# A state-space scan's decay tiles: exponents of both directions joined before one exponential

## The chip, the cores and the metric

One core of one Trainium2 chip runs the whole program. The metric is the device time of one execution in microseconds (us), the median of several runs. TensorE (PE) multiplies matrices, VectorE (DVE), ScalarE (ACT) and GpSimd (POOL) work on elements, SyncE (SP) issues the weight loads.

## The reference, cut to what matters

Two transformer-like blocks over 256 tokens of width 1024. The part of this case is the first block's bidirectional state-space scan: 8 groups of 4 heads, two chunks of 128 tokens, one scan forwards and one backwards over the same `b`, `c` and `x`:

```python
decay = segsum_exp(a_dt)      # exp(cs[l] - cs[s]) where l >= s, else 0
cb = jnp.einsum('bclgn,bcsgn->bcgls', c, b)
y_diag = jnp.einsum('bcgls,bcgrls,bcsgrp->bclgrp', cb, decay, xdt)
...
y = y_fwd + y_bwd + xs * d_skip.astype(jnp.float32).reshape(G, R, 1)
```

With s on the partitions and l along the free axis, the forward scan fills the entries l >= s of a tile, the backward scan the entries l <= s, and both fill the diagonal l = s, where the exponential of each is 1 (times its own dt).

## The kernel before, in words

All weights come as a stream of 147 pieces of 1 MB. Piece s belongs to slot s. For each slot SP loads `raw`, ACT copies it rounded to `w_hi` (`split_hi`, L1068), DVE subtracts (`w_lo`, `split_lo`, L1452), and PE multiplies the activations with both, three products each (`three`, L393). PE handles slot s in two halves of 12 matmuls of 512 columns each. ACT and DVE run two slots ahead (`AHEAD = 2`) with their splits: in their loop over s they split piece s + 2, and ACT may do so once PE has finished slot s - 1. Each engine follows its own list in program order and waits only on semaphores.

The scan lies in slots 27 to 36, the last of the z projection and the first of the gate projection; group g is worked on in slot 28 + g. Each PSUM bank has a pair of counters: PE `claim`s a bank by waiting until its last user has drained it; `ready` waits until PE has filled it, `emptied` until it is drained. For every group:

- After slot 27 + g, PE computes `ssd_cb(g)` (L884, bank 7) and `ssd_decay(g, 0)`; in the middle of slot 28 + g it computes `ssd_decay(g, 1)` (`slot_middle`, L897), and after that, for group g - 1, `ssd_states` (L852), `ssd_diagonal` (L843, bank 4) and `ssd_across` (L893, bank 7).
- `ssd_decay(g, c)` writes the exponents of a tile of 128 x 512 (4 heads) for the forward direction into bank 5 and for the backward one into bank 6. For each it issues a matmul of `cum_s` with `cum_l` (L865), and a second one (L867) that adds -1e30 on the half that the direction does not have: `unit` (an identity) times `far` (the mask).
- ACT copies `cb` (L1227), takes the exponentials of both banks for c = 0 (`decay_exps`, L1149, L1157), splits the weights of slot s + 2, does the squares of group g - 2 (L1316), the exponentials for c = 1, and the copy of `state` (L1323). In slots 28 and 30 it also applies Silu to a z chunk (L1329), so its function tables are exchanged.
- DVE in slot 28 + g: `ssd_weigh(g, 0)` (L1702: add the two exponentials, L1706, multiply with `cb`, L1709), `split_lo` (L1455), `ssd_weigh(g, 1)`, `ssd_gate(g - 1)` (L1713: times `d_skip`, L1720; `y_off`, L1724, which frees bank 7 for the next `ssd_cb`; three more, L1728 to L1736), and after every second gate slot `gate_bias` (L1743).
- POOL makes `x_state` (L2069) and the rows `cum_s` of the next group (L2078).

Of the kernel before, what the change touches and what calls it, by code (L numbers as in the profile page):

```python
# [33 lines left out]
P = 128  # L34
TOK = 256
# [112 lines left out]
def build(nc, w_stream, w_dt, x_in, params_in, table_in, onehot_in, gate_bias_in, post_in, rpb_in,  # L148
# [3 lines left out]
    with ctx:  # L152
# [106 lines left out]
        decay_back = [at(f"decay_back{c}", [P, PER_GROUP, P], 150592 + 2048 * c) for c in range(RT)]  # L259
        cb = at("cb", [P, RT, P], 154688)  # L260
        far = at("far", [P, 2, P], 141376, F32R)
        ndt = at("ndt", [P, RT, 2 * HEADS], 158272)
        unit = at("unit", [P, P], 158784, F32R)
# [68 lines left out]
        decay_scaled, far_ready, x_state_ready = sem("decay_scaled"), sem("far_ready"), sem("x_state_ready")  # L332
# [40 lines left out]
        def _(pe):  # L373
# [482 lines left out]
            def ssd_decay(g, c):  # L856


                pe.wait_ge(cum_s_ready, g + 1)
                if g == 0 and c == 0:  # L860
                    pe.wait_ge(far_ready, 1)
                for d in range(2):
                    key = ("decay", g, c, d)
                    claim(key, 5 + d)
                    pe.matmul(ps[:, 5 + d, :], cum_s[g % 2][:, 2 * c + d, :], cum_l[c][:, d, :, :],  # L865
                              start=True, stop=False)
                    pe.matmul(ps[:, 5 + d, :], unit[:, :], far[:, d].unsqueeze(1).to_broadcast([P, PER_GROUP, P]),  # L867
                              start=False, stop=True).then_inc(*fill_of(key))
# [28 lines left out]
            def slot_middle(s):  # L897

                if 0 <= s - 10 < 8:
                    values1(s - 10)  # L900
                if 0 <= s - 97 < 4:
                    values2(s - 97)
                if s in TURN_AT:
                    conv_turn(TURN_AT[s])
                if 0 <= s - 28 < GROUPS:
                    ssd_decay(s - 28, 1)
                if 0 <= s - 29 < GROUPS:
                    ssd_states(s - 29)
                    ssd_diagonal(s - 29)
                    ssd_across(s - 29)  # L910
# [148 lines left out]
        def _(act):  # L1059
# [89 lines left out]
            def decay_exps(g, c):  # L1149
                for d, dest in enumerate((decay[g % 2][c], decay_back[c])):  # L1150
                    key = ("decay", g, c, d)
                    ready(act, key)
                    if d == 0 and g >= 2:
                        ready(act, ("y", g - 2))
                    if d == 1 and g:
                        act.wait_ge(decay_scaled, 2 * g - 1 + c)
                    act.activation(dest[:, :, :], ps[:, 5 + d, :].rearrange("p (h l) -> p h l", h=PER_GROUP),  # L1157
                                   ACT.Exp).then_inc(*drain_of(key))
# [60 lines left out]
            for s in range(SLOTS):  # L1219
                if 0 <= s - 28 < GROUPS:  # L1220
                    g = s - 28
                    key = ("cb", g)
                    ready(act, key)
                    if g:

                        act.wait_ge(decay_scaled, 2 * g)
                    act.activation(cb[:, :, :], ps[:, 7, 0:2 * P].rearrange("p (c l) -> p c l", c=2),  # L1227
                                   ACT.Copy).then_inc(*drain_of(key))
                    decay_exps(g, 0)
# [3 lines left out]
                if s == S_Q2 - 2:  # L1233
                    split_hi(S_Q2 + 1)
                name, form, chunk, part, opens, closes = slots[s]
# [82 lines left out]
                if 0 <= s - 28 < GROUPS:  # L1318
                    decay_exps(s - 28, 1)
                if 0 <= s - 29 < GROUPS:  # L1320
# [3 lines left out]
                                   ACT.Copy).then_inc(*drain_of(key))  # L1324
                if name == "z" and closes:
# [117 lines left out]
        def _(dve):  # L1443
# [257 lines left out]

            def ssd_weigh(g, c):  # L1702

                emptied(dve, ("decay", g, c, 0)), emptied(dve, ("decay", g, c, 1))
                w = decay[g % 2][c]
                link(dve.tensor_tensor(w[:, :, :], w[:, :, :], decay_back[c][:, :, :], ALU.add))  # L1706
                if c == 0:
                    emptied(dve, ("cb", g))
                dve.tensor_tensor(w[:, :, :], w[:, :, :],  # L1709
                                  cb[:, c, :].unsqueeze(1).to_broadcast([P, PER_GROUP, P]),  # L1710
                                  ALU.mult).then_inc(decay_scaled, 1)

            def ssd_gate(g):  # L1713
# [4 lines left out]
                for c in range(RT):  # L1718
                    v = xtok(c, g * GW, GW).rearrange("p (h d) -> p h d", h=PER_GROUP)
                    ins = dve.tensor_tensor(v, v, per_head(param("d_skip")[:, 4 * g:4 * g + 4], 4), ALU.mult)  # L1720
                link(ins)
                ready(dve, ("off", g))
# [97 lines left out]
            for s in range(SLOTS):  # L1820
                if 0 <= s - 28 < GROUPS:
                    ssd_weigh(s - 28, 0)
# [61 lines left out]
                if s == 18:  # L1884
                    decay_tables()
                if 0 <= s - 28 < GROUPS:
                    ssd_weigh(s - 28, 1)
# [149 lines left out]
        def _(pool):  # L2037
# [36 lines left out]
            def decay_rows(g):  # L2074

                if g >= 2:
                    ready(pool, ("decay", g - 2, 1, 0))
# [4 lines left out]
            pool.tensor_copy(unit[:, :], ident)  # L2082
# [3 lines left out]
            pool.wait_ge(conv_silu, 7)  # L2086
            pool.tensor_scalar(far[:, :, :], tri[:, 2:4], NEG, None, ALU.mult).then_inc(far_ready, 1)
# [14 lines left out]
            ready(pool, ("decay", GROUPS - 1, 1, 0))  # L2102
# [128 lines left out]
```

## Time and profile before

| | us |
|---|---|
| median of 3 runs | 943.63 (942.15 to 943.77) |
| the profiled execution | 942.23 |
| its span, first to last instruction | 940.4 |
| PE busy | 932.4 (99%) |
| DVE busy | 662.4 (70%) |
| ACT busy | 507.6 (54%) |
| POOL busy | 60.8 (6%) |

An instruction's duration is not the distance to the next one: matmuls and element operations overlap their neighbours' ends. Where many of one kind follow each other, the distance from start to start is what one of them costs its engine. An f32 matmul (not rounded) has two records in the trace. Only one execution has a trace, and its times are given from the start of its span.

### The profile page before, as it was taken

The page shows a single profiled execution, that of the slowest core. Times are in us where ns is not written, and L with a number is a line of the kernel's source. Part 1 is how long each engine was busy: PE and PEld are TensorE (multiplying, and loading weights), DVE is VectorE, ACT ScalarE, POOL GpSimd, SP SyncE. Part 2 cuts the span into 40 slices and gives each one's busy share as a digit, 9 for nine tenths or more (in the row PEclk, how much of TensorE's full clock was granted, in tenths as well). Part 3 has the DMA queues.
Part 4 walks back from the last instruction along what each step waited for, and adds up shares of the span by engine and source line. Part 5 has one row for each costly group of instructions (what it writes and reads, how often), then busy time and mean ns, then how long its engine had stood idle before and what let it go on. Part 6 is the DMA issues. An engine that isn't in the chain of part 4 may idle for free.

```text
span 940.4 us, 13246 instructions
## 1 busy us (share of the span) xinstructions
PE 932.4 (99%) x5362; PEld 807.9 (86%) x5362; DVE 662.4 (70%) x946; ACT 507.6 (54%) x664; POOL 60.8 (6%) x68
## 2 busy tenths in 40 slices
PE   9999999999999999999999999999999999999998
PEld 8988899988888888888888888899888898888887
DVE  6779789998878764778776446767665758776433
ACT  6457876676555733456554335755653455554331
POOL 1000000023321000000003310000000000000000
PEclk9999999999999999999999999999999999999999
DMA  8943233554224475435447955353355435546551
GB/s 306 341 168 124 93 133 135 180 167 169 91 90 157 140 307 197 169 131 221 179 180 236 256 196 206 136 205 128 123 217 179 179 135 217 187 179 224 178 179 45
DMA packets 25278, 166.51 MB, mean 177 GB/s; under 512 B 2987, under 2 KB 3115, under 8 KB 6657
## 3 DMA queue, kind: packets, MB, share of 16 engines
q1 hardware_dynamic: 22464, 156.12, 46.1%
q0 software_dynamic: 2752, 9.54, 3.5%
q8 instruction: 43, 0.70, 0.3%
q14 instruction: 19, 0.15, 0.0%
HBM read 164.57 MB, written 1.08 MB: 176 GB/s over the span
## 4 chain that ended last, share of the span: by engine, by line
PE 86%; DVE 11%; ACT 2%; issue 1%; ACTq 0%; DVEq 0%
PE ps L393 54%; PE ps L582 11%; PE ps L587 6%; DVE conv_acc L1688 5%; DVE w_lo L1455 3%; PE ps L843 1%; PE ps L772 1%; PE ps L787 1%; PE ps L424 1%; PE ps L426 1%; PE ps L433 1%; PE ps L512 1%; PE ps L630 1%; PE ps L893 1%; PE ps L852 1%
## 5 line engine op out<-in xcount | busy, mean ns | idle before, releaser
L1455 DVE TENSOR_TENSOR w_lo<-raw,w_hi 128x2048 fp32r<-128x2048 f32 x145 | 331.3, 2291 | 181.0 <-ACT w_hi L1075 180.8
L1075 ACT ACTIVATE w_hi<-raw 128x2048 fp32r<-128x2048 f32 x145 | 275.5, 1906 | 179.1 <-PE ps L393 160.2
L393 PE MATMUL ps<-w_hi,ht 128*128 128x512 f32 (+1 forms) x576 | 181.4, 388 | 0.0
L393 PE MATMUL ps<-ht,w_hi 128*128 128x256 f32 (+1 forms) x816 | 150.6, 286 | 0.0
L393 PEld LDWEIGHTS ps<-ht,w_hi 128*128 128x128 f32 (+1 forms) x816 | 126.2, 190 | 4.1 <-issue 4.0
L393 PEld LDWEIGHTS ps<-w_hi,ht 128*128 128x128 f32 x576 | 107.3, 188 | 22.4 <-issue 1.1
L393 PE MATMUL ps<-ht,w_lo 128*128 128x256 f32 (+1 forms) x408 | 115.3, 282 | 0.0
L393 PE MATMUL ps<-w_lo,ht 128*128 128x512 f32 (+1 forms) x288 | 110.5, 384 | 0.0
L582 PE MATMUL ps<-ht,w_hi 128*128 128x512 f32 x448 | 109.5, 391 | 0.0
L393 PE MATMUL ps<-w_hi,ff_hi 128*128 128x512 f32 x256 | 99.7, 389 | 0.0
L393 PE MATMUL ps<-w_lo,ff_hi 128*128 128x512 f32 x256 | 99.6, 389 | 0.0
L393 PE MATMUL ps<-w_hi,ff_lo 128*128 128x512 f32 x256 | 99.6, 389 | 0.0
L582 PEld LDWEIGHTS ps<-ht,w_hi 128*128 128x128 f32 x448 | 81.5, 189 | 15.2
L393 PEld LDWEIGHTS ps<-ht,w_lo 128*128 128x128 f32 (+1 forms) x408 | 77.6, 190 | 0.0
L393 PEld LDWEIGHTS ps<-w_lo,ht 128*128 128x128 f32 x288 | 54.2, 188 | 10.4
L587 PEld LDWEIGHTS ps<-ht,w_lo 128*128 128x128 f32 x448 | 59.3, 191 | 3.3
L587 PE MATMUL ps<-ht,w_lo 128*128 128x256 f32 x448 | 60.3, 282 | 0.0
L393 PEld LDWEIGHTS ps<-w_hi,ff_hi 128*128 128x128 f32 x256 | 48.1, 188 | 10.0
L393 PEld LDWEIGHTS ps<-w_hi,ff_lo 128*128 128x128 f32 x256 | 48.0, 188 | 10.0
L393 PEld LDWEIGHTS ps<-w_lo,ff_hi 128*128 128x128 f32 x256 | 48.1, 188 | 9.8
L1688 DVE SCALAR_TENSOR_TENSOR conv_acc<-conv_in,params,conv_acc 128x256 f32<-128x256 f32 x128 | 52.1, 477 | 0.0
L1190 ACT ACTIVATE ff_sum<-ps 128x512 f32<-128x512 f32 x32 | 18.8, 595 | 35.4 <-PE ps L587 34.4
(301 smaller groups left out, 1217.4 us busy)
## 6 DMA issues: line engine op xcount, KB each, us to landing
raw<-in_w_stream SPq DMA_DIRECT2D x145, 1024.0 KB, 4.8
bias<-rel_scratch POOLq DMA_DIRECT2D x1, 3072.0 KB, 21.2
bias<-in_rpb POOLq DMA_DIRECT2D x16, 128.0 KB, 7.9
x_first<-in_x_in SPq DMA_DIRECT2D x2, 512.0 KB, 4.1
raw<-in_w_stream SPq DMA_DIRECT2D x2, 512.0 KB, 6.4
gates<-in_gate_bias POOLq DMA_DIRECT2D x4, 256.0 KB, 6.0
gates<-in_gate_bias POOLq DMA_DIRECT2D x2, 512.0 KB, 7.2
x<-in_x_in POOLq DMA_DIRECT2D x1, 1024.0 KB, 5.3
```

Of the source, the lines that this page charges most:

```text
L393: ins = pe.matmul(o, still, moving, start=first and n == 0, stop=last and n == 2, skip_group_check=True)
L424: pe.matmul(ps[:, i, 0:TOK], hi[:, c], ht_hi[:, k, :], start=opens and kt == 0, stop=False, skip_group_check=True)
L426: pe.matmul(ps[:, i, 0:TOK], lo[:, c], ht_hi[:, k, :], start=False, stop=False, skip_group_check=True)
L433: ins = pe.matmul(ps[:, i, TOK:2 * TOK], hi[:, kt * 512 + i * P:kt * 512 + i * P + P], ht_lo[:, 4 * part + kt, :], start=False, stop=close ...
L512: pe.matmul(ps[:, bank0 + r, :], ht_hi[:, 4 * part + kt, tokens], w[:, kt * 512:kt * 512 + 512], start=part == 0 and kt == 0 and m == 0, s ...
L582: pe.matmul(ps[:, 4 * (chunk % 2) + i, :], hi[:, cols(kt, i)], ht[:, :, 4 * part + kt, :], start=opens and kt == 0, stop=False, skip_group ...
L587: ins = pe.matmul(ps[:, 4 * (chunk % 2) + i, 0:TOK], lo[:, cols(kt, i)], ht_hi[:, 4 * part + kt, :], start=False, stop=closes and kt == 3, ...
L630: pe.matmul(ps[:, 2 * n + r, :], a_hi[:, kt, r * P:r * P + P], w[:, cols], start=kt == 0 and m == 0, stop=False, skip_group_check=True)
L1075: act.activation(split_home(s)[0][:, 0:width(s)], raw[s % RAW_RING][:, 0:width(s)], ACT.Copy).then_inc(hi_ready, 1)
L1190: act.activation(ff_sum[half][:, :, :], ps[:, b:b + 2, TOK:2 * TOK], ACT.Copy).then_inc(lows_out, 1)
L1455: dve.tensor_tensor(lo[:, 0:width(s)], raw[s % RAW_RING][:, 0:width(s)], hi[:, 0:width(s)].bitcast(F32), ALU.subtract).then_inc(lo_ready, 1)
L1688: ins = dve.scalar_tensor_tensor(acc_of(c)[:, i, :], conv_in[k][:, i, tap:tap + TOK], conv_w[:, tap, f:f + 1], acc_of(c)[:, i, :], ALU.mul ...
```

## The change

Bank 5 gets the forward exponents and bank 6 the backward ones, with no mask product. DVE copies bank 6 over bank 5 where s > l (`ssd_choose`, a predicated copy with the mask `tri[:, 2]`), which drains bank 6. ACT then takes one exponential of bank 5, which drains it, and DVE multiplies with `cb`; the add is gone. The diagonal now holds the forward share alone. The backward share is `dt` of the backward direction times the row product of b and c: DVE multiplies b and c once (`twins`, 128 x 2048), 16 matmuls of one column sum over the partitions (`twin_sums`, bank 4), and `own_terms` adds the result to `d_skip`, giving `own_skip`, by which `ssd_gate` multiplies in place of `d_skip`. On ACT the exponential for c = 0 now stands behind the weight split of its slot, and the one for c = 1 behind the copy of `state`. On DVE the multiplication for c = 1 moves into `ssd_gate` of the group before, behind its skip product. POOL no longer makes `unit` and `far`.

```diff
@@ -256,11 +256,10 @@
         gates = at("gates", [P, RT, 2 * D], 192352)
         decay = [[at(f"decay{i}_{c}", [P, PER_GROUP, P], 142400 + 4096 * i + 2048 * c) for c in range(RT)]
                  for i in range(2)]
-        decay_back = [at(f"decay_back{c}", [P, PER_GROUP, P], 150592 + 2048 * c) for c in range(RT)]
+        twins = at("twins", [P, GROUPS, TOK], 146496)
         cb = at("cb", [P, RT, P], 154688)
-        far = at("far", [P, 2, P], 141376, F32R)
         ndt = at("ndt", [P, RT, 2 * HEADS], 158272)
-        unit = at("unit", [P, P], 158784, F32R)
+        own_skip = at("own_skip", [P, RT, HEADS], 158784)
 
         adt_wide = at("adt_wide", [P, 4, 4, HEADS], 175968)
         ndt_wide = at("ndt_wide", [P, 4, 4, HEADS], 184160)
@@ -857,15 +856,22 @@
 
 
                 pe.wait_ge(cum_s_ready, g + 1)
-                if g == 0 and c == 0:
-                    pe.wait_ge(far_ready, 1)
                 for d in range(2):
                     key = ("decay", g, c, d)
                     claim(key, 5 + d)
                     pe.matmul(ps[:, 5 + d, :], cum_s[g % 2][:, 2 * c + d, :], cum_l[c][:, d, :, :],
-                              start=True, stop=False)
-                    pe.matmul(ps[:, 5 + d, :], unit[:, :], far[:, d].unsqueeze(1).to_broadcast([P, PER_GROUP, P]),
-                              start=False, stop=True).then_inc(*fill_of(key))
+                              start=True, stop=True).then_inc(*fill_of(key))
+
+            def twin_sums():
+
+                claim("twins", 4)
+                pe.wait_ge(twins_ready, 1)
+                for c in range(RT):
+                    for g in range(GROUPS):
+                        at0 = c * GROUPS + g
+                        ins = pe.matmul(ps[:, 4, at0:at0 + 1], twins[:, g, c * P:c * P + P], tri[:, 0, P - 1:P],
+                                        start=True, stop=True)
+                ins.then_inc(*fill_of("twins"))
 
             def cumulate():
 
@@ -904,6 +910,8 @@
                     conv_turn(TURN_AT[s])
                 if 0 <= s - 28 < GROUPS:
                     ssd_decay(s - 28, 1)
+                    if s == 28:
+                        twin_sums()
                 if 0 <= s - 29 < GROUPS:
                     ssd_states(s - 29)
                     ssd_diagonal(s - 29)
@@ -1147,15 +1155,14 @@
                 ins.then_inc(exp_ready, 1)
 
             def decay_exps(g, c):
-                for d, dest in enumerate((decay[g % 2][c], decay_back[c])):
-                    key = ("decay", g, c, d)
-                    ready(act, key)
-                    if d == 0 and g >= 2:
-                        ready(act, ("y", g - 2))
-                    if d == 1 and g:
-                        act.wait_ge(decay_scaled, 2 * g - 1 + c)
-                    act.activation(dest[:, :, :], ps[:, 5 + d, :].rearrange("p (h l) -> p h l", h=PER_GROUP),
-                                   ACT.Exp).then_inc(*drain_of(key))
+                key = ("decay", g, c, 0)
+                emptied(act, ("decay", g, c, 1))
+                if g == 1 and c == 0:
+                    ready(act, "twins")
+                if g >= 2:
+                    ready(act, ("y", g - 2))
+                act.activation(decay[g % 2][c][:, :, :], ps[:, 5, :].rearrange("p (h l) -> p h l", h=PER_GROUP),
+                               ACT.Exp).then_inc(*drain_of(key))
 
             def values_hi(a):
                 r, tile = a // 4, 2 * (a % 4)
@@ -1226,12 +1233,13 @@
                         act.wait_ge(decay_scaled, 2 * g)
                     act.activation(cb[:, :, :], ps[:, 7, 0:2 * P].rearrange("p (c l) -> p c l", c=2),
                                    ACT.Copy).then_inc(*drain_of(key))
-                    decay_exps(g, 0)
                 late = s in (S_MI - 1, S_MI2 - 1)
                 if s + AHEAD < SLOTS and s != S_Q2 - 1 and not late:
                     split_hi(s + AHEAD)
                 if s == S_Q2 - 2:
                     split_hi(S_Q2 + 1)
+                if 0 <= s - 28 < GROUPS:
+                    decay_exps(s - 28, 0)
                 name, form, chunk, part, opens, closes = slots[s]
                 if s == 0:
                     ready(act, "rel")
@@ -1315,13 +1323,13 @@
                             act.wait_ge(gsq_ready, 2 * g + c)
                         act.activation(junk[:, :], xtok(c, g * GW, GW), ACT.Square,
                                        accum_out=gstat[:, 0, 2 * g + c:2 * g + c + 1]).then_inc(gsq_ready, 1)
-                if 0 <= s - 28 < GROUPS:
-                    decay_exps(s - 28, 1)
                 if 0 <= s - 29 < GROUPS:
                     key = ("state", s - 29)
                     ready(act, key)
                     act.activation(state[:, :, :], ps[:, 7, :].rearrange("p (a b) -> p a b", a=2),
                                    ACT.Copy).then_inc(*drain_of(key))
+                if 0 <= s - 28 < GROUPS:
+                    decay_exps(s - 28, 1)
                 if name == "z" and closes:
                     for r in range(RT):
                         key = ("z", chunk, r)
@@ -1699,16 +1707,35 @@
 
                 return values.unsqueeze(2).to_broadcast([P, count, HD])
 
+            def ssd_choose(g, c):
+
+                ready(dve, ("decay", g, c, 0)), ready(dve, ("decay", g, c, 1))
+                both = [ps[:, 5 + d, :].rearrange("p (h l) -> p h l", h=PER_GROUP) for d in range(2)]
+                dve.copy_predicated(both[0], tri[:, 2].bitcast(I32).unsqueeze(1).to_broadcast([P, PER_GROUP, P]),
+                                    both[1]).then_inc(*drain_of(("decay", g, c, 1)))
+
             def ssd_weigh(g, c):
 
-                emptied(dve, ("decay", g, c, 0)), emptied(dve, ("decay", g, c, 1))
-                w = decay[g % 2][c]
-                link(dve.tensor_tensor(w[:, :, :], w[:, :, :], decay_back[c][:, :, :], ALU.add))
+                emptied(dve, ("decay", g, c, 0))
                 if c == 0:
                     emptied(dve, ("cb", g))
+                w = decay[g % 2][c]
                 dve.tensor_tensor(w[:, :, :], w[:, :, :],
                                   cb[:, c, :].unsqueeze(1).to_broadcast([P, PER_GROUP, P]),
                                   ALU.mult).then_inc(decay_scaled, 1)
+
+            def own_terms():
+
+                ready(dve, "twins")
+                v = own_skip[:, :, :].rearrange("p c (g h) -> p c g h", g=GROUPS)
+                for c in range(RT):
+                    ins = dve.tensor_tensor(v[:, c], dt[:, c, HEADS:2 * HEADS].rearrange("p (g h) -> p g h", g=GROUPS),
+                                            ps[:, 4, c * GROUPS:c * GROUPS + GROUPS].unsqueeze(2)
+                                            .to_broadcast([P, GROUPS, PER_GROUP]), ALU.mult)
+                ins.then_inc(*drain_of("twins"))
+                emptied(dve, "twins")
+                link(dve.tensor_tensor(own_skip[:, :, :], own_skip[:, :, :],
+                                       param("d_skip").unsqueeze(1).to_broadcast([P, RT, HEADS]), ALU.add))
 
             def ssd_gate(g):
 
@@ -1717,8 +1744,10 @@
                 dve.wait_ge(x_state_ready, 2 * (g + 1))
                 for c in range(RT):
                     v = xtok(c, g * GW, GW).rearrange("p (h d) -> p h d", h=PER_GROUP)
-                    ins = dve.tensor_tensor(v, v, per_head(param("d_skip")[:, 4 * g:4 * g + 4], 4), ALU.mult)
+                    ins = dve.tensor_tensor(v, v, per_head(own_skip[:, c, 4 * g:4 * g + 4], 4), ALU.mult)
                 link(ins)
+                if g + 1 < GROUPS:
+                    ssd_weigh(g + 1, 1)
                 ready(dve, ("off", g))
                 for i in range(RT):
                     ins = dve.tensor_tensor(y_off[:, i].rearrange("p (h d) -> p h d", h=PER_GROUP),
@@ -1819,7 +1848,7 @@
 
             for s in range(SLOTS):
                 if 0 <= s - 28 < GROUPS:
-                    ssd_weigh(s - 28, 0)
+                    ssd_choose(s - 28, 0)
                 if 0 <= s - 10 < 8:
                     values_lo(s - 10)
                 if s in TURN_AT:
@@ -1883,8 +1912,16 @@
                                     .unsqueeze(2).to_broadcast([P, 4, 2, HEADS])).then_inc(adt_wide_ready, 1)
                 if s == 18:
                     decay_tables()
+                if s == 27:
+                    dve.wait_ge(conv_silu, 8)
+                    dve.tensor_tensor(twins[:, :, :], bc[:, 0:GROUPS, :], bc[:, GROUPS:2 * GROUPS, :],
+                                      ALU.mult).then_inc(twins_ready, 1)
                 if 0 <= s - 28 < GROUPS:
-                    ssd_weigh(s - 28, 1)
+                    ssd_weigh(s - 28, 0)
+                    ssd_choose(s - 28, 1)
+                if s == 28:
+                    ssd_weigh(0, 1)
+                    own_terms()
                 if s == S_GATE + 5:
                     dve.wait_ge(gate_bias_second, 32)
                     gate_bias(1)
@@ -2074,17 +2111,14 @@
             def decay_rows(g):
 
                 if g >= 2:
-                    ready(pool, ("decay", g - 2, 1, 0))
+                    ready(pool, ("decay", g - 2, 1, 1))
                 pool.tensor_scalar(cum_s[g % 2][:, :, :], cum[:, :, :], quad[:, 10 + g:11 + g],
                                    quad[:, 18 + g:19 + g], ALU.mult, ALU.add).then_inc(cum_s_ready, 1)
 
             pool.wait_ge(params_landed, 16)
-            pool.tensor_copy(unit[:, :], ident)
             pool.wait_ge(tables_ready, 1)
             decay_rows(0)
 
-            pool.wait_ge(conv_silu, 7)
-            pool.tensor_scalar(far[:, :, :], tri[:, 2:4], NEG, None, ALU.mult).then_inc(far_ready, 1)
             pool.wait_ge(conv_silu, 8)
             pool.wait_ge(state_scaled, 1)
             for c in range(6):
@@ -2099,7 +2133,7 @@
                 if g + 1 < GROUPS:
                     decay_rows(g + 1)
             pool.wait_ge(cum_s_ready, GROUPS)
-            ready(pool, ("decay", GROUPS - 1, 1, 0))
+            ready(pool, ("decay", GROUPS - 1, 1, 1))
             for cols, done in ((slice(512, 1024), gate_bias_second), (slice(1024, 2 * D), gate_bias_rest)):
                 for r in range(RT):
                     pool.dma_start(gates[:, r, cols], gate_bias_in[cols].partition_broadcast(P)).then_inc(done, 16)
```

## Rows read from the trace of the kernel before

**Rows 1.** The page: busy time of TensorE, and its granted clock in 40 slices.
```profile
PE 932.4 (99%) x5362; PEld 807.9 (86%) x5362; DVE 662.4 (70%) x946; ACT 507.6 (54%) x664; POOL 60.8 (6%) x68
...
PEclk9999999999999999999999999999999999999999
```

**Rows 2.** Chain of waits, 200 to 300 us: start us, us, what.
```profile
223.72 0.23 PE ps L865
223.96 0.23 PE ps L867
...
252.07 1.73 PE ps L843 x16
...
262.51 0.86 PE ps L852 x4
263.38 1.73 PE ps L843 x16
265.11 0.92 PE ps L893 x4
266.02 2.76 PE ps L393 x12
```

**Rows 3.** Waits, 196 to 300 us: engine line <- releaser: total us, times, longest us.
```profile
PEld ps L884 <- DVE y_off L1724: 0.8, 1, 0.8
PE ps L884 <- DVE y_off L1724: 0.4, 1, 0.4
```

**Rows 4.** Groups by shape, 203 to 298 us: count | busy us, mean ns | idle before.
```profile
L1706 DVE TENSOR_TENSOR decay<-decay,decay_back 128x512 f32<-128x512 f32 x16 | 14.2, 885 | 11.0 <-ACT decay_back L1157 11.0
...
L867 PE MATMUL ps<-far,unit 128*128 128x512 f32 x32 | 12.6, 393 | 0.0
```

**Rows 5.** Timeline of TensorE about the middle of slot 28: start us, us, instruction.
```profile
207.47 0.40 PE L865 MATMUL ps<-cum_l,cum_s 128*128 128x512 f32 x1
```

**Rows 6.** Timeline of DVE in the first scan slots.
```profile
204.36 2.46 DVE L1455 TENSOR_TENSOR w_lo<-raw,w_hi 128x2048 fp32r<-128x2048 f32 x1 [0.73 <-ACT w_hi L1075]
...
208.83 2.30 DVE L1455 TENSOR_TENSOR w_lo<-raw,w_hi 128x2048 fp32r<-128x2048 f32 x1
211.04 0.68 DVE L1706 TENSOR_TENSOR decay<-decay,decay_back 128x512 f32<-128x512 f32 x1
```

**Rows 7.** One line's instructions: the DVE addition that reads PSUM.
```profile
L1728 DVE TENSOR_TENSOR xtok<-ps,xtok x8: 681/681/682, 222.9 to 298.5; 128x512 f32<-128x512 f32 x8
```

**Rows 8.** Timeline of TensorE: matmuls of 32 columns, and what follows.
```profile
68.03 0.98 PE L831 MATMUL ps<-adt,params 128*128 128x32 f32 x8
68.84 0.63 PE L787 MATMUL ps<-params,logit 128*128 128x128 f32 x4
```

**Rows 9.** Timeline of ACT in slots 29 and 32.
```profile
212.95 1.28 ACT L1157 ACT_TABLE_LOAD   x1
214.24 0.60 ACT L1157 ACTIVATE decay<-ps 128x512 f32<-128x512 f32 x1
...
246.62 0.38 ACT L1227 ACTIVATE cb<-ps 128x256 f32<-128x256 f32 x1 [4.49 <-PE ps L884]
247.09 0.60 ACT L1157 ACTIVATE decay<-ps 128x512 f32<-128x512 f32 x1
...
248.06 1.92 ACT L1075 ACTIVATE w_hi<-raw 128x2048 fp32r<-128x2048 f32 x1
249.87 0.41 ACT L1316 ACTIVATE junk<-xtok 128x256 f32<-128x256 f32 x1
```

**Rows 10.** Stretches: us, then busy us (instructions) of PE, PEld, DVE, ACT, POOL; clock; DMA.
```profile
240.00:300.00 60.00, 59.98 (x322) 51.84 (x321) 51.26 (x70) 28.49 (x57) 18.50 (x18) 1.00 0.39 132
```

**Rows 11.** Timeline of ACT in the second block: a table load ahead of a wait.
```profile
635.15 1.28 ACT L1143 ACT_TABLE_LOAD   x1
637.14 0.51 ACT L1143 ACTIVATE logit<-logit,soft 128x256 f32<-128x256 f32 x1 [0.71 <-DVE soft L1618]
```

**Rows 12.** Start of the span, TensorE: the first matmuls, after idle.
```profile
1.45 5.49 PE L915 MATMUL ps<-warm 128*128 128x512 f32 x12 [1.45 <-DVE warm L1474]
```

More of the change, by code:

```diff
@@ L331, in build @@
         ndt_ready = sem("ndt_ready")
-        decay_scaled, far_ready, x_state_ready = sem("decay_scaled"), sem("far_ready"), sem("x_state_ready")
+        decay_scaled, twins_ready, x_state_ready = sem("decay_scaled"), sem("twins_ready"), sem("x_state_ready")
         pool_chain = sem("pool_chain")
```

## The prediction

> **What bounds the kernel now.** I read the page first: TensorE is busy for 932.4 of 940.4 us, at a granted clock of 1.00 in every slice [rows 1]. So time is won only where TensorE's own list gets shorter, and lost wherever it is made to wait. Then I read the chain of waits over the scan, 200 to 300 us. Up to 223 us it runs through DVE and ACT (weight splits, exponentials, at last `y_off`), from there on it is TensorE alone, matmul behind matmul, L867 among them [rows 2]. The list of waits agrees: in the whole scan TensorE waits once, for `y_off`, 0.8 us by its weight loads (0.4 by the matmuls, whose ends are modelled) [rows 3]. So before 223 us a saving on TensorE is hidden in part by DVE, and afterwards it counts in full, as long as DVE and ACT keep up.
>
> **What is removed.** Of TensorE: 32 mask matmuls (L867). A duration of 393 ns [rows 4] isn't their price, since neighbours overlap; from start to start one takes 0.23 us (223.72 to 223.96 for L865, the same shape) [rows 2]. 32 x 0.23 = **-7.4 us** of TensorE's list. Of ACT: 16 exponentials of 0.6 us [rows 9]; ACT is busy 28.5 of 60 us in the scan [rows 10], so by itself this is worth nothing to the end. Of DVE: 16 additions (mean 885 ns [rows 4]), in whose place come 16 predicated copies. Of POOL: two mask preparations that nobody waits for behind 204 us. The table loads stay as many: Exp, Silu, Exp, Silu, Exp.
>
> **What is added to TensorE.** 16 f32 matmuls with a moving side of one column, each with its own 128 x 128 weights, two records each, so 32. No row has one column. The nearest: eight records with 32 columns take 68.84 - 68.03 = 0.81 us, 0.10 each [rows 8]; sixteen with 64 columns take 1.73 us, 0.108 each [rows 2]. Halving the columns moved it by 0.007 us, so the weight load sets the price: 32 x 0.104 = **+3.3 us**. Bounds: 3.5 us by the 64-column row; below, if half of the 0.10 went with the columns, 1.6 us. I take 3.3. They stand in slot 28 on TensorE's list and nothing hides them if TensorE is the bound there, which the next step makes it.
>
> **The new wait in slot 28.** Before, the two matmuls of `ssd_decay(0, 1)` start at 207.47 us, right behind the first half of slot 28 [rows 5]. Without two mask matmuls (0.46 us) TensorE would be there at 207.0. But bank 5 is now free only after: `w_lo` of piece 29 (ends 206.8 [rows 6]), the product `twins` (128 x 2048, the size of `w_lo`, whose next neighbour starts 2.2 us later: 208.83 to 211.04 [rows 6]), the predicated copy, and one exponential (0.6 us). The predicated copy isn't in the trace. Nearest is the DVE addition with one side in PSUM, 0.68 us [rows 7]; that is my value. Bounds: 0.5 us if it does no more than stream 512 elements at the pace at which 2048 take 2.2 us, and 1.4 us if it passed twice. 206.8 + 2.2 + 0.7 + 0.6 and two hand-overs of 0.05 make 210.4: TensorE idles **+3.4 us** (3.2 to 4.1). The Exp table load doesn't lie in this sum: where one wait stands ahead of an activation, the load goes first, as in the second block, where it ran at 635.15 and the activation still waited for DVE until 637.14 [rows 11]. Were it held, 1.3 us more. Behind it on TensorE are the one-column matmuls and the second half of slot 28; ACT and DVE then wait for those (`z`, `ssd_cb(1)`), so the lateness is carried on whole. Where before there was a wait for `y_off` at 223 us, TensorE is now late by itself and the 0.8 us of that wait are swallowed: **-0.8 us**.
>
> **The new wait in each later slot.** TensorE gives ACT half a slot, 12 matmuls or 2.76 us (the last of [rows 2]), between the matmuls for c = 0 and those for c = 1. In that time ACT must do: `cb` (0.47 us to its neighbour), the weight split (1.81), one exponential (0.6) [rows 9], from the end of `ssd_cb`, which is 0.46 us before the half starts. 0.47 + 1.81 + 0.6 = 2.9 against 2.76 + 0.46 = 3.2: it fits with 0.3 us to spare, no wait. In slots 29 and 31 there is a table load of 1.28 us [rows 9] between split and exponential, because Silu ran in the slots before. That makes 4.2 against 3.2, and with `cb` a little late behind the z copies I take 1.2 us: twice, **+2.4 us**. Before, the load stood there too, but the split stood behind the exponentials: 0.4 + 1.28 + 1.1 = 2.8 us, which fitted.
>
> DVE was busy 51.3 of the 60 us from 240 on [rows 10]. A slot took 263.38 - 252.07 = 11.3 us [rows 2], so that is 9.7 us of DVE per slot. Two additions of 0.885 [rows 4] give way to two copies of 0.68: 9.3 us, against TensorE's new slot of 11.3 - 0.9 = 10.4. DVE isn't the bound. On DVE `ssd_weigh(g, 1)` now stands ahead of `y_off` and waits for the exponential for c = 1; queued behind it is `y_off`, for which `ssd_cb(g + 1)` waits. TensorE gives it 0.86 + 1.73 + 0.92 + 2.76 = 6.3 us after the matmuls for c = 1 [rows 2]. Copy 0.7, `state` and exponential 1.2, multiplication 0.7 are done before `ssd_across` ends at 3.5; then `y_off` with 0.8 makes 4.3. It is hidden, with 2 us as the cover. `own_terms` (three small ones on DVE, under 1 us) is wanted by `ssd_diagonal(0)` a slot later: nothing. SP's queue and its loads don't move, except that they follow `w_lo`, which is two slots ahead.
>
> **The sum.** -7.4 + 3.3 + 3.4 - 0.8 + 2.4 = **+0.9 us**. The profiled execution took 942.23 us, so 943.1 by its measure; it lies 1.4 us below the median of 943.63, and I give the forecast on the median: 943.63 + 0.9 = **944.5 us**. A difference below 0.2%, 1.9 us, can't be told from none here. With the bounds above: the one-column matmuls at 1.6 give -1.7, the copy at 0.5 gives -0.2, at 1.4 it gives +0.7 in slot 28 and, in slots where `gate_bias` makes DVE late, some tenths each, up to +2 in all. So the likeliest case spans 942.6 to 946.5 us.
>
> **The page on table loads.** In the trace the exponential starts 0.01 us after the load has ended (212.95 + 1.28, then 214.24) [rows 9]. The Trainium skill (ScalarE: Activation LUTs, "What ACT_TABLE_LOAD costs") says that 1283 ns of load are followed by a drain of 1380 ns, 2.66 us together. By that page the two waits of slots 29 and 31 would be 2.8 us longer together, an estimate of 947.3; the row doesn't bear the drain out, at least not as time that ACT loses, so I give it no chance of its own.
>
> **Rivals.** *Slower, by the clock (15%).* TensorE stands still for 3.4 us and then has 3.3 us of one-column matmuls, the emptiest stretch of the program. At the start of the span, after idling, twelve matmuls of 512 columns took 5.49 us, 0.46 each instead of 0.23, the lower of the two levels (1.2 GHz) [rows 12]. If the level falls in slot 28, the second half of that slot costs 2.8 us more and the small matmuls up to 3.3: with +0.9 it makes 947.3 to 950.6, say 949. It decides once the granted clock between 207 and 220 us reads below 1.00. Against it: all rows of the granted clock read 1.00, with shorter gaps only. The Trainium skill (TensorE: Matmul & The Clock Gate, "What's actually happening") holds that an idle array is put back to the lower level and work raises it again; [rows 12] agree with the second part, and no row here shows a fall.
>
> *Slower, by DVE (15%).* If the predicated copy takes over 1.2 us because both its sides are in PSUM, 16 of them put another 16 x 0.5 = 8 us on DVE, 1.0 per slot. DVE then needs 10.3 of 10.4 us and every hand-over that had 0.3 us to spare becomes a wait of some tenths in most slots: +2.5 to +4 in all, 947. For it: the trace has no such operation. Against: every DVE operation with one side in PSUM goes at the same pace as one without ([rows 6, 7]).
>
> *Faster, the waits absorbed (15%).* If the one-column matmuls cost half (1.6 us) and the two table loads go ahead of the split's end or of their wait, so that slots 29 and 31 hide them, -7.4 + 1.6 + 3.4 - 0.8 + 0.4 = -2.8, 940.8 us. For it: in slot 29 ACT idles ahead of the second half. Against: the split stands ahead of the load on ACT's list, and it can't begin before TensorE has finished the slot before.
>
> *The mask matmuls weren't worth their time:* that they were hidden is excluded after 223 us by the chain [rows 2], where 24 of the 32 lie.
>
> **Chances.** Forecast 55%, clock 15, DVE 15, faster 15. Of the forecast's case some 47 lie within 0.2%, 6 above and 2 below; of the rival by DVE 3 of 15 lie within, of the faster one 1 of 15. Faster by over 0.2%: 0.16; within: 0.51; slower: 0.33. The range 942.0 to 948.5 leaves out most of the faster case and most of the clock case.
>
> **What would show it.** Right: 32 records fewer at the place of L867, 32 new ones of about 0.10 us; one idle time of TensorE near 207 to 210 us for an exponential, two of about 1 us near 221 and 243 us for the first exponential of their slots; all other slots at 10.4 us; the predicated copy at 0.68 us. Wrong: no idle at 207 us, an idle time in every slot (then the split in front of the exponential is the cause), a granted clock below 1.00, or a copy of over 1 us.

## The result, and the profile after

The changed kernel takes 949.39 us (median of 4 runs, 947.27 to 950.25), the kernel before 942.89 beside it (942.10 to 943.77): 1.0066 times as long by the comparison of all runs, 95% interval 1.0053 to 1.0079. The profiled execution took 950.25 us, the longest of the four; its span is 948.4. The forecast was 944.5 us with a range up to 948.5; the measured time lies above both.

The page after shows TensorE busy for 935.1 us, 99% of the span. Of its granted clock (before: [rows 1]) one slice, 213 to 237 us, isn't 9:

```profile
PEclk9999999997999999999999999999999999999999
```

Stretches of the same execution: busy us (instructions) of PE, PEld, DVE, ACT, POOL; then the granted clock. It reads 1.00 up to 207 us, falls to the lower level, 1.2 GHz, within the first row, stays there over the second and comes back within the third:

```profile
207.00:214.00 7.00, 3.79 (x18) 3.62 (x17) 6.34 (x6) 2.21 (x4) 2.40 (x1) 0.74 0.94 275
214.00:221.00 7.00, 7.00 (x27) 6.32 (x28) 0.71 (x4) 1.37 (x2) 0.00 (x0) 0.50 0.31 132
221.00:228.00 7.00, 6.33 (x24) 4.91 (x22) 2.33 (x2) 4.42 (x5) 0.00 (x0) 0.79 0.00 0
```

TensorE in slots 28 and 29, timeline (before: [rows 5]). The last matmul ahead of `ssd_decay(0, 1)` ends at 207.0, then TensorE waits 3.21 us for the exponential, then has the 32 one-column records:

```profile
206.62 0.39 PE L392 MATMUL ps<-w_hi,ht 128*128 128x512 f32 x1
210.22 1.12 PE L862 MATMUL ps<-cum_l,cum_s 128*128 128x512 f32 x2 [3.21 <-ACT decay L1164]
211.14 6.82 PE L872 MATMUL ps<-params,twins 128*128 128x1 f32 x32
217.82 0.77 PE L392 MATMUL ps<-w_hi,ht 128*128 128x512 f32 x1
...
228.39 0.70 PE L862 MATMUL ps<-cum_l,cum_s 128*128 128x512 f32 x2 [1.06 <-ACT decay L1164]
```

The records take 217.82 - 211.14 = 6.7 us, 0.21 each, twice the 0.104 of the forecast. The chain of waits gives the second half of slot 28 and a later slot (before: [rows 2]); the same 12 matmuls take 5.33 us there and 2.78 later, and a slot at full clock now takes 262.57 - 252.13 = 10.4 us, as forecast:

```profile
217.96 5.33 PE ps L392 x12
...
243.03 2.78 PE ps L392 x12
...
252.13 1.73 PE ps L842 x16
...
262.57 1.73 PE ps L842 x16
```

The new DVE operation and the waits (before: [rows 3, 7]). The predicated copy takes 0.69 us; in the whole scan TensorE waits three times for the one exponential, 5.4 us in all, where the sum put 3.4 + 2.4:

```profile
L1714 DVE COPY_PREDICATED ps<-params,ps x16: 681/692/697, 208.8 to 294.6; 128x512 f32<-128x512 int32 x16
```
```profile
PE ps L862 <- ACT decay L1164: 5.4, 3, 3.2
```

So the waits, the copy and the length of the later slots stand in the trace near their forecast size; what the sum has no term for is the clock. The experiments try three theories of its fall. A: the wait in slot 28 alone brings it down. C: the one-column matmuls alone do. B: either leaves TensorE idle or nearly so, and what counts is the whole emptier stretch, wait and one-column matmuls together.

### The profile page after: what moved, and what is told of

It is laid out like the page before. It is cut to its first block, busy times and chain, and to the rows that moved or that the text cites. A ratio compares the mean times of both kernels' runs of the same rounds, so it can differ in the third digit from the quotient of the medians.

```text
span 948.4 us, 13221 instructions
## 1 busy us (share of the span) xinstructions
PE 935.1 (99%) x5362; PEld 810.3 (85%) x5362; DVE 660.4 (70%) x950; ACT 500.2 (53%) x648; POOL 50.5 (5%) x66
## 4 chain that ended last, share of the span: by engine, by line
PE 85%; DVE 11%; ACT 2%; issue 1%; DMA 0%; SPq 0%; ACTq 0%; DVEq 0%
PE ps L392 54%; PE ps L581 11%; PE ps L586 6%; DVE conv_acc L1696 5%; DVE w_lo L1463 3%; PE ps L842 1%; PE ps L771 1%; PE ps L786 1%; PE ps L423 1%; PE ps L425 1%; PE ps L432 1%; PE ps L511 1%; PE ps L862 1%; PE ps L899 1%; PE ps L629 1%
## 5 line engine op out<-in xcount | busy, mean ns | idle before, releaser
L392 PE MATMUL ps<-w_hi,ht 128*128 128x512 f32 (+1 forms) x576 | 183.4, 392 | 0.0
```

Of the source, the lines that this page charges most:

```text
L392: ins = pe.matmul(o, still, moving, start=first and n == 0, stop=last and n == 2, skip_group_check=True)
```

## Experiments

Each time is a median over 4 to 11 executions, beside executions of the kernel before on the same chip. These took 942.34 us beside the first four kernels, 942.23 beside the two with 128 columns in slot 28 and the last two of this section, and 942.27 beside the others. The kernel before itself has two levels: of its 61 executions 47 took 942.0 to 942.5 us, and 14 took 943.5 to 943.8 at a mean clock of 0.998 (7 of 25, 4 of 27 and 3 of 9 in the three comparisons). A single short fall of the clock, worth about 1.5 us, is thus no property of the change. Below, "undisturbed" means runs with a mean clock of 1.000 or 0.999; for the kernel before they take 942.2 to 942.3 us. The sums of the first four expectations start from 942.9, which is 0.6 us more.

**Product without sums.** The sums go, and `own_terms` is one copy (the waits for the sums, cut here, go with them):

```diff
-                    if s == 28:
-                        twin_sums()
+                link(dve.tensor_copy(own_skip[:, :, :], param("d_skip").unsqueeze(1).to_broadcast([P, RT, HEADS])))
```

> The changed kernel without the 16 one-column matmuls (own_skip is a copy of d_skip, so the backward share of the diagonal is left out of the result); the product of b and c stays on DVE, and with it TensorE's wait of 3.2 us in slot 28. Theory A (the granted clock falls because of the wait alone): the clock reads 0.5 for some time behind the wait, and the time is 943 to 946 us. Theory B (it falls because of the wait and the one-column matmuls together) and theory C (because of the one-column matmuls alone): the clock reads 1.00 throughout and the time is the one before (942.9) - 7.4 + 3.2 + 2.2 - 0.8 = 940.1 us.

942.04 us. TensorE still waits 3.2 us. The mean clock is 0.998 or less in eight of ten runs, and in the profiled one it reads 0.83 over 210 to 220 us. So a wait is enough to bring the clock down, for less time than in the changed kernel. But the run with a mean clock of 1.000 took 941.81 us, as long as those with 0.998 (941.75 to 942.16): one short fall costs nothing here; only the two runs at 0.996 took longer, 942.9 and 943.3. Something else sets the time. It is 1.7 us more than the 940.1 of the expectation, and 2.3 us more if that sum starts from the kernel before beside it. The chain of waits shows what ends last:

```profile
213.00 0.60 ACT decay L1160
...
213.61 1.28 ACT L1333
...
215.91 0.38 ACT cb L1230
216.29 1.81 ACT w_hi L1081
...
218.12 1.28 ACT L1160
...
219.41 0.60 ACT decay L1160
...
220.15 0.70 PE ps L862 x2
```

From `ssd_decay(0, 1)` to `ssd_decay(1, 1)` ACT has in a row: exponential, Silu table, z, `cb`, split, Exp table, exponential. The forecast counted this from `cb` on, with the z copies as a small lateness. With the sums on TensorE's list this chain is covered by them: with the clock at 1.00 in both, the wait in slot 29 is 1.09 us with them (**Both**, below) and 2.41 without them or the product (**Neither**).

**Sums without the product:**

```diff
-                    dve.tensor_tensor(twins[:, :, :], bc[:, 0:GROUPS, :], bc[:, GROUPS:2 * GROUPS, :],
-                                      ALU.mult).then_inc(twins_ready, 1)
...
-                        ins = pe.matmul(ps[:, 4, at0:at0 + 1], twins[:, g, c * P:c * P + P], tri[:, 0, P - 1:P],
+                        ins = pe.matmul(ps[:, 4, at0:at0 + 1], bc[:, g, c * P:c * P + P], tri[:, 0, P - 1:P],
```

> The changed kernel without the product on DVE; the 16 one-column matmuls take b itself as weights (so the own share is not the reference's). TensorE's wait in slot 28 shrinks by 2.2 us to about 1.1. Theories A and B: clock 1.00, 32 records at 0.10 us, 942.9 - 7.4 + 1.1 + 3.3 + 2.2 - 0.8 = 941.3 us. Theory C: the clock reads 0.5 from within the one-column matmuls on, which then take up to 0.2 us per record, and the time is 944 to 947 us.

945.16 us, and three levels: 943.6 to 943.8 (mean clock 0.998), 945.1 to 945.4 (0.996), 946.8 to 946.9 (0.995). The first wait is 1.2 us only, yet no run has a mean clock above 0.998, and six of ten are lower than any of the kernel before. In the profiled run it reads 0.66 over 210 to 220 us. A is out as the whole cause.

**Neither:** both edits.

> The changed kernel with neither the product nor the one-column matmuls (the backward share of the diagonal is left out): the joined exponents alone. All theories: clock 1.00; a wait of 1.1 us in slot 28 and of 1.1 us in slots 29 and 31: 942.9 - 7.4 + 3.3 - 0.8 = 938.0 us. If it is above 940, steps other than those of the twins cost time and the sum of the prediction is wrong in them.

939.86 us; six of ten runs 939.6 to 939.9 at a clock of 1.000 or 0.999, the others 941.5 to 943.2 with a fall. The number of falls, four of ten, is no evidence by itself beside 7 of 25 of the kernel before. But three of the four are longer than any of that kernel (mean clock 0.996, 3.2 to 3.4 us of time), and in the profiled run the clock reads 0.57 over 218 to 222 us, right behind the wait in slot 29. So waits of 1.25 and 2.41 us (slots 28 and 29) can bring a fall.

Undisturbed, the joined exponents alone are worth 939.7 - 942.3 = -2.6 us; the expectation's sum says -4.9. Of the 2.3 us between them 1.3 is the wait in slot 29 (2.41 against 1.1), by the ACT chain. The rest is spread over smaller terms; one is the masks (see below, why the prediction was wrong). Product: 941.8 - 939.7 = 2.1 us, as forecast (2.2).

**The kernel before without the masks:**

```diff
-                              start=True, stop=False)
-                    pe.matmul(ps[:, 5 + d, :], unit[:, :], far[:, d].unsqueeze(1).to_broadcast([P, PER_GROUP, P]),
-                              start=False, stop=True).then_inc(*fill_of(key))
+                              start=True, stop=True).then_inc(*fill_of(key))
...
-                                   ACT.Exp).then_inc(*drain_of(key))
+                                   ACT.Exp, scale=0.0).then_inc(*drain_of(key))
```

> The kernel before without its 32 mask matmuls (L867), nothing else moved; the exponentials are taken with scale 0, so that the unmasked exponents stay finite, and the decays are all 1. If a mask matmul costs TensorE 0.23 us and those before 223 us are hidden by DVE: 24 x 0.23 = 5.5, 937.4 us; if all 32 count: 935.5 us; if the wait for y_off at 223 us grows by what was saved ahead of it and DVE then sets the pace in later slots too: above 939 us.

938.30 us (938.21 to 938.43), clock 1.00 in all four runs: 4.0 us gained, not 5.5 or 7.4. New waits of TensorE stand where there had been one: 1.2 us for `state`, 0.9 for an exponential, 0.7 for `y_off`. Even without the change's own waits nearly half of the 7.4 us is lost again to others.

**Wait filled** (the `claim` moves here from `twin_sums`):

```diff
+                if s == 28:
+                    claim("twins", 4)
+                    for _ in range(14):
+                        pe.matmul(ps[:, 4, :], cum_s[0][:, 0, :], cum_l[0][:, 0, :, :], start=True, stop=True)
```

> The changed kernel with 14 matmuls of 512 columns (14 x 0.23 = 3.2 us) into bank 4 on TensorE's list ahead of the matmuls that wait in slot 28; their result is overwritten by the one-column sums. Nothing is released earlier or later, only the wait is filled with work. Theory A (the fall of the clock comes from the wait): clock 1.00, the one-column records at 0.10 us, and the time is the predicted sum, 943.2 to 943.9 us. Theory C (from the one-column matmuls): the clock falls within or behind them all the same, in one to three stretches of 3.4 us at 1.7 us each, 945 to 948 us. If only the length of the whole emptier stretch counts (theory B): in between, fewer stretches at 0.5 than the changed kernel.

945.53 us: one run 943.92 at a clock of 1.000, three at 945.4 to 945.6, two at 947. TensorE had no idle time in slot 28, and the profiled execution shows the clock at 0.66 over 210 to 220 us all the same, from within the one-column records. So they bring the fall too. But 3.9 us of the 949.4 are gone with the wait, though its time is still spent.

**Sums with 128 columns**:

```diff
-                        ins = pe.matmul(ps[:, 4, at0:at0 + 1], twins[:, g, c * P:c * P + P], tri[:, 0, P - 1:P],
+                        ins = pe.matmul(ps[:, 4, at0:at0 + P], twins[:, g, c * P:c * P + P], tri[:, 0, P - 1:P].to_broadcast([P, P]),
```

> The changed kernel, but each of the 16 sums moves 128 equal columns instead of one (the later ones overwrite all but the first column of the earlier, so the result is the same). By the rows of 128 columns a record costs 0.11 us, so the list of TensorE grows by 0.2 us only, but its columns are no longer empty. The wait of 3.2 us in slot 28 stays. If the fall of the clock hangs on the array being idle (wait) or nearly so (one column) (theory B): it now falls as the kernel without sums does, one stretch or none: 944 to 945.5 us. If it hangs on the wait alone (A): as the changed kernel, 949. If on some other property of the sums (f32, weight loads): as the changed kernel, 949.

945.58 us, ratio to before 1.0038 (1.0026 to 1.0051), against 1.0066 with one column. More columns, less time. All five runs still have a fall (mean clock 0.998, one 0.996); the next experiment shows that it belongs to the wait.

**Both** (the wait filled, the sums with 128 columns):

> The wait filled with 14 matmuls and the sums with 128 columns: TensorE is never idle or nearly idle in slot 28. Theory B: the clock reads 1.00 there in every run, and all runs lie where the forecast's sum put them, 943.2 to 944.1 us, against 942.3 before. If a run still shows a low stretch, the reason lies outside slot 28 (waits of slots 29 and 31), or theory B is wrong.

944.07 us, ratio 1.0021 (1.0012 to 1.0030): eight of eleven runs 943.84 to 944.13 at a clock of 1.000, three at 945.5 with 0.998, about as often as the kernel before (14 of 61). The stretch with the end of the filled wait, the sums and the second half of slot 28 in its profiled execution, columns as above:

```profile
210.00:220.00 10.00, 10.00 (x63) 8.71 (x62) 4.81 (x8) 5.27 (x7) 0.00 (x0) 1.00 0.58 222
```

TensorE's list is 3.4 us longer than the changed kernel's (0.2 of it by the columns, the rest inside the wait). What it waits for comes no earlier: `ssd_decay(0, 1)` starts at 210.29 us and not 210.22, and the waits in slots 29 and 31 are 1.09 us each, in the changed kernel 1.06 and 1.09. Yet it is 5.3 us faster. That is the price of the clock, shown. Of the theories A and C are each out as the whole cause. B is what the runs bear out: the wait with full sums, or the one-column sums with the wait filled, each leave shorter falls, and with neither none are left beyond those of the kernel before.

**The exponential ahead of the split again, from group 1 on** (an edit of the changed kernel, as all that follow):

```diff
+                    if g:
+                        decay_exps(g, 0)
...
-                if 0 <= s - 28 < GROUPS:
-                    decay_exps(s - 28, 0)
+                if s == 28:
+                    decay_exps(0, 0)
```

> The changed kernel with ACT's exponential for c = 0 ahead of the weight split again, from group 1 on. The waits of TensorE in slots 29 and 31 (1.1 us each) go, the wait of 3.2 us in slot 28 and the one-column matmuls stay. If the two waits cost what the trace shows: 949.4 - 2.2 = 947.2 us at the same length of low clock. If they are hidden or taken over by a later split: no change within 0.5 us.

954.72 us, 5 us worse than the change where 2 better or no difference was expected. (The profiled execution had a clock of 0.95 in stretches far from the scan too and took 954.11; the others, at 0.991 to 0.995, took 953.2 to 957.0.) DVE in slot 33, timeline:

```profile
258.34 0.69 DVE L1716 COPY_PREDICATED ps<-params,ps 128x512 f32<-128x512 int32 x1
261.49 2.29 DVE L1465 TENSOR_TENSOR w_lo<-raw,w_hi 128x2048 fp32r<-128x2048 f32 x1 [2.47 <-ACT w_hi L1083]
```

Copy, exponential, split, `w_lo` go one after the other, so DVE idles about 2.5 us in each slot and becomes the bound: from slot to slot it now takes 11.45 us, where TensorE's own list needs 10.4. The change's order, split first, is a needed part of it.

**Halves of the sums in slots 29 and 31**, behind the matmuls for c = 1 (product of four groups at the end of DVE's slots 28 and 30, `twins` of half the size, `own_terms` ahead of `ssd_gate`):

```diff
+                    if s in (29, 31):
+                        twin_sums((s - 29) // 2)
```

> The changed kernel with the product and the sums in two halves: product of groups 0 to 3 on DVE behind its work of slot 28, sums in the middle of slot 29; groups 4 to 7 in slots 30 and 31. The wait of slot 28 shrinks from 3.2 to 1.1 us, ahead of it nothing is emptier; the eight matmuls (16 records, 1.7 us) stand alone. Theories A and B: no or one stretch at low clock; time = that of the kernel with neither product nor sums (939.7 us in its undisturbed runs) + 3.3 = 943.0, less what the wait of 2.4 us in slot 29 gives back if the product is done by then. Theory C: two falls, 945 to 946 us.

949.75 us, no better than the change. In the profiled execution the clock is 0.50 over 220 to 230 us: it falls behind a wait of 2.4 us in slot 29 with 16 one-column records on it, and the rest of that slot is slow. In slot 31, behind a wait of 1.1 us, the other 16 bring no fall; the clock reads 1.00, and they take 248.92 - 247.22 = 1.70 us:

```profile
247.22 1.84 PE L873 MATMUL ps<-params,twins 128*128 128x1 f32 x16
248.92 1.11 PE L851 MATMUL ps<-x_state,btok 128*128 128x256 f32 x4
```

The same with the exponential first and the copy for c = 1 ahead of the split in slot 28:

> The same, and in addition the exponential for c = 0 ahead of the split from group 1 on, and in slot 28 DVE's copy for c = 1 ahead of its split. The waits in slots 29 and 31 go. 942.3 - 7.4 + 1.1 (wait in slot 28) + 3.3 (sums) - 0.8 = 938.5 us, with the clock at 1.00, so faster than the kernel before by 0.4%. If the clock falls at the one-column matmuls (theory C), 940 to 942.

958.79 us; the error of the exponential again, with falls in slots 29 and 31. Here it also makes `own_terms` late, which stand behind the split on DVE's list: TensorE waits 2.5 and 2.2 us for `own_skip` in these two slots.

**Halves, with 128 columns, ahead of the matmuls that wait:**

```diff
+                if s in (29, 31):
+                    twin_sums((s - 29) // 2)
                 if 0 <= s - 28 < GROUPS:
                     ssd_decay(s - 28, 1)
```

> Product and sums in two halves, the sums with 128 columns, and placed ahead of the matmuls that wait in slots 29 and 31, so that they fill those waits (2.4 and 1.1 us) with 1.75 us of work each. Against the kernel with neither product nor sums (939.7 us without a fall): + 0 in slot 29, + 0.65 in slot 31: 940.4 us, 0.2% faster than the kernel before. If the clock falls as often as there (4 of 10 runs): some runs 1.5 to 3 us above.

941.07 us, ratio 0.9992 (0.9983 to 1.0001): eight of eleven runs at 941.0 to 941.15, clock 0.999 to 1.000. Against the kernel with halves above (949.75) only the columns and the place are changed; which of the two gives how much of the 8.7 us was not tried.

**And the copy for c = 1 first in slot 28:**

```diff
                     ssd_choose(s - 28, 0)
+                if s == 28:
+                    ssd_choose(0, 1)
```

> As before, and in slot 28 DVE's copy for c = 1 ahead of its weight split, so that the chain through ACT (exponential, Silu table, z, cb, split, Exp table, exponential) that ends the wait in slot 29 begins 1.5 us earlier. TensorE's wait in slot 29 shrinks until the sums (1.75 us) fill it: 940.4 - 0.7 = 939.7 us. If the split, now later, is what ACT and DVE lack in the next slot: no gain or a loss of some tenths.

940.73 us, ratio 0.9985 (0.9976 to 0.9994): faster than both kernels, by 1.5 us than the one before. That is a small gain, but its interval leaves out 1. TensorE, timeline: the sums now stand where it waited, and of 2.4 us of idle 0.35 is left:

```profile
215.16 1.95 PE L873 MATMUL ps<-params,twins 128*128 128x128 f32 x16
217.46 0.70 PE L862 MATMUL ps<-cum_l,cum_s 128*128 128x512 f32 x2 [0.35 <-ACT decay L1163]
```

## Why the prediction was wrong

- **The step that failed** is that the sum priced everything at the full clock: a wait of 3.4 us, one-column matmuls of 3.3 us, and nothing for the work behind them, as if an idle TensorE had no after-effect. The fall of the clock was left to a rival of 15%. It is what happened. In the profiled run the sums took 6.7 us and not 3.4, and the second half of slot 28 took 5.33 and not 2.77: 3.3 + 2.6 = 5.9 us. Between the medians with and without the fall it is 949.39 - 944.07 = 5.3 us.
- **The rival's price** of 949 us had the mechanism and both sizes (2.8, and up to 3.3) right. That it met 949.39 so closely is in part luck: it took about half of the second size, and its base of 943.63 lay 1.4 us above the undisturbed kernel before, since two of the three runs behind that median were of the upper level.
- **Why 15% was too low.** Against the rival stood that all rows read a granted clock of 1.00. But outside the start no wait of TensorE in the kernel before is longer than 1.1 us, so these rows couldn't tell. And at the start the record of the clock itself is in doubt: it reads 1.00 over 2 to 4 us, where the twelve matmuls of [rows 12] ran at half pace. Either it misses a low level there, or that pace had another cause; no run tells. The kernel before, its columns as above:

```profile
2.00:4.00 2.00, 2.00 (x6) 1.56 (x5) 0.00 (x0) 0.01 (x1) 0.00 (x0) 1.00 0.96 326
```

- **Without the clock the sum held within 1 us.** With the wait filled, undisturbed runs took 943.8 to 944.1 us, 1.8 more than the kernel before beside them; the sum said +0.9.
- **Wait in slot 28:** 3.21 us, forecast 3.4. Waits in slots 29 and 31: 1.06 and 1.09, forecast 1.2 each. The table load in slot 28 ran ahead of its wait, as forecast: load at 206.22, exponential at 209.48. Predicated copy 0.69 us, forecast 0.68; the rival by DVE is out, though DVE became the bound once ACT's order was turned.
- **One-column records:** priced right in their own time. At full clock 16 of them take 1.70 us, 0.106 each, where the forecast had 0.104.
- **Two terms were off and partly cancelled.** The joined exponents alone were dearer than the sum by 2.3 us, 1.3 of it by the ACT chain from slot 28 to 29. The sums cost 1.0 us less than their own time of 3.3, since they cover that chain: +1.8 with them, -0.5 without them and with the product. That is luck of the place; the forecast had given nothing for it.
- **The masks:** where TensorE is the bound, a slot takes 10.44 us and not 11.31, so the saving is 8 x 0.87 = 7.0 us and not 7.4. In the kernel before the same removal gives only 4.0, as other waits take over.
- **The faster rival** needed the waits absorbed. They can be, with work put into them, as the last two kernels show. That wasn't what the change did.
- What stays open: why one-column matmuls behind an unfilled wait bring falls of such different length from run to run (mean clock 0.992 to 0.996), and where in the program the single short fall of the kernel before lies; its profiled execution had none.

## What to carry over

When an edit makes a TensorE that is otherwise never idle wait for some microseconds, or gives it many matmuls of one column, price the work behind it at the lower clock level too, and not as an unlikely rival, even if no earlier row shows a fall: here 3.2 us of waiting and 3.4 us of one-column sums cost 5.3 us on top. Not every wait does it: in the last two kernels, with waits of 1.2 to 1.3 us and sums of 128 columns, 5 of 22 runs had a short fall, as often as the kernel before. In this kernel a sum by matmul with one useful column was better moved with 128 equal ones, and put where TensorE waits anyhow. Where an engine's result goes through a second engine and back (PE, DVE, ACT, PE), follow its whole list from the last such hand-over, table loads included, not only from the slot's first instruction.

## What was not expected of the hardware

- With waits of 1.25 and 2.41 us on TensorE and no one-column matmuls, three of ten runs had a longer fall of the clock (0.996) than any of 61 runs of the kernel before (0.998).
- More columns made a kernel faster: 949.4 to 945.6 us by moving 128 columns in place of one, at the same wait.
- 14 needless matmuls of 512 columns in the wait took the one-column kernel from 949.4 to 945.5 us, and the 128-column one from 945.6 to 944.1.
